# Grouped-query attention inside a fused encoder layer: both key-value heads in one piece, scores and products with v on alternating halves of the TensorE array

## The reference, cut to what matters

```python
def sink_attention(q, k, v, valid, sinks):
    s = jnp.einsum('...qhgd,...khd->...hgqk', q, k,
                   preferred_element_type=jnp.float32) * (ATTN_HEAD_DIM ** -0.5)
    if valid is not None:
        s = jnp.where(valid[..., None, None, None, :], s, -jnp.inf)
    sink = sinks.astype(jnp.float32).reshape(ATTN_KV_HEADS, ATTN_GROUP, 1, 1)
    m = jnp.maximum(jnp.max(s, axis=-1, keepdims=True), sink)
    p = jnp.exp(s - m)
    w = p / (jnp.sum(p, axis=-1, keepdims=True) + jnp.exp(sink - m))
    return jnp.einsum('...hgqk,...khd->...qhgd', w.astype(v.dtype), v)
```

## Time and profile before

| | |
|---|---|
| median of 3 runs | 1014.32 us (1013.77 to 1015.25) |
| the profiled execution, its own time | 1015.18 us |
| its span, first to last instruction | 1013.5 us |
| mean granted TensorE clock | 0.996 |
| TensorE busy | 992.2 us, 98% of the span |
| VectorE, ScalarE, GpSimd busy | 62%, 39%, 8% |

### The profile page before, as it was taken

The page is one execution under the profiler, slowest core; times in us unless marked ns, Lnnn a source line. Parts: engine busy times, 40 slices in busy tenths (PEclk is TensorE's granted clock), DMA queues, the critical chain, the costliest instruction groups (busy, mean ns, idle before and its releaser), DMA issues.

```text
span 1013.5 us, 19083 instructions
## 1 busy us (share of the span) xinstructions
PE 992.2 (98%) x7220; PEld 960.9 (95%) x7220; DVE 632.5 (62%) x1244; ACT 399.7 (39%) x693; POOL 85.8 (8%) x140
## 2 busy tenths in 40 slices
PE   6999999999999999999999899999999999999997
PEld 5999989898999999999999899999999999999997
DVE  5545665766666643434548789724997369965762
ACT  4324433423343522222544455423454135443252
POOL 1022212112110000000001200000000000030000
PEclk9999999999999999999999999999999999999999
DMA  7434212212221222244702513521234213365211
GB/s 206 125 111 128 80 55 64 63 53 67 68 65 56 65 87 83 72 126 132 220 22 84 215 55 94 158 83 43 84 101 129 84 43 114 89 225 155 84 46 49
DMA packets 166197, 98.45 MB, mean 97 GB/s; under 512 B 14656, under 2 KB 162528, under 8 KB 165872
## 3 DMA queue, kind: packets, MB, share of 16 engines
q1 hardware_dynamic: 159904, 79.19, 27.6%
q0 software_dynamic: 4336, 16.67, 4.6%
q10 hardware_dynamic: 1888, 1.64, 0.5%
HBM read 86.79 MB, written 10.75 MB: 96 GB/s over the span
## 4 chain that ended last, share of the span: by engine, by line
PE 91%; DVE 4%; issue 2%; ACT 2%; DMA 1%; DVEq 0%; SPq 0%; ACTq 0%
PE acc L679 34%; PE acc L935 10%; PE acc L937 10%; PE acc L936 10%; PE small L935 6%; PE small L936 6%; PE small L937 6%; PE small L807 2%; PE small L822 2%; PE small L850 1%; PE small L854 1%; PE small L759 1%; PE small L852 1%; PE small L1088 1%; DMA x_row<-in_x_sample 1%
## 5 line engine op out<-in xcount | busy, mean ns | idle before, releaser
L679 PE MATMUL acc<-xh,whi 128*128 128x288 f32 x736 | 163.1, 303 | 1.6 <-DVE wlo L1599 1.5
L679 PE MATMUL acc<-xl,whi 128*128 128x288 f32 x736 | 157.4, 295 | 0.0
L679 PE MATMUL acc<-xh,wlo 128*128 128x288 f32 x736 | 157.1, 294 | 0.0
L1116 ACT ACTIVATE whi<-raw 128x1024 fp32r<-128x1024 f32 (+1 forms) x62 | 62.1, 1001 | 198.3 <-PE acc L679 198.3
L1599 DVE TENSOR_TENSOR wlo<-raw,whi 128x1024 fp32r<-128x1024 f32 (+1 forms) x64 | 74.3, 1162 | 81.1 <-ACT whi L1116 77.8
L679 PEld LDWEIGHTS acc<-xh,whi 128*128 128x128 f32 x736 | 116.8, 189 | 8.5 <-issue 7.4
L679 PEld LDWEIGHTS acc<-xh,wlo 128*128 128x128 f32 x736 | 118.1, 188 | 0.0
L679 PEld LDWEIGHTS acc<-xl,whi 128*128 128x128 f32 x736 | 118.0, 188 | 0.0
L1906 DVE TENSOR_TENSOR wlo<-raw,whi 128x512 fp32r<-128x512 f32 (+2 forms) x93 | 81.0, 872 | 49.6 <-ACT whi L1327 33.8
L935 PE MATMUL acc<-yh,whi 128*128 128x288 f32 x360 | 107.2, 298 | 1.3 <-DVE wlo L1906 1.3
L937 PE MATMUL acc<-yh,wlo 128*128 128x288 f32 x360 | 106.1, 295 | 0.0
(11 more groups left out here) (312 smaller groups left out, 2376.9 us busy)
## 6 DMA issues: line engine op xcount, KB each, us to landing
raw<-in_w_in SPq DMA_DIRECT2D x92, 256.0 KB, 3.2
raw<-in_w_ffn_gate SPq DMA_DIRECT2D x44, 256.0 KB, 3.4
raw<-in_w_ffn_up SPq DMA_DIRECT2D x44, 256.0 KB, 4.0
raw<-in_w_ffn_down SPq DMA_DIRECT2D x32, 256.0 KB, 3.6
res<-x_scratch POOLq DMA_DIRECT2D x16, 288.0 KB, 4.3
raw<-in_w_branch_ret SPq DMA_DIRECT2D x16, 256.0 KB, 2.9
raw<-in_w_out SPq DMA_DIRECT2D x16, 256.0 KB, 4.4
raw<-in_w_ffn_down SPq DMA_DIRECT2D x16, 192.0 KB, 3.6
```

The costliest lines, as they stand in the source:

```text
L679: ins = nc.tensor.matmul(acc[:, a, hf, 0:HALF], w[:, s, at:at + P], x(k)[:, hf * HALF:(hf + 1) * HALF], start=first and n == 0 and m == 0, ...
L1116: nc.scalar.activation(whi[:, s, 0:n], raw[:, s, 0:n], ACT.Copy).then_inc(hi_ready, 1)
```

## The change

A round of pieces now takes two query heads of both key-value heads (round `p`: query heads 2p and 2p+1 of each). The score tiles stand in the order head 0, head 1, head 0, head 1, so that successive matmuls contract over partitions 0 to 63 and 64 to 127 in turn; head 0's scores go to the first bank of `att`, head 1's to the second. The products with v are two matmuls for each tile of keys, of half the moving columns, one to output partitions 0 to 63 and one to 64 to 127. ScalarE takes the result out in one copy over 128 partitions and half the columns. VectorE's reads of the sinks are re-indexed. The table `PLACES` and all semaphores' counts stay.

```diff
--- before.py
+++ after.py
@@ -792,20 +792,25 @@
             for n in (2, 3):
                 run_unit(unit(U_Q + n), unit(J_Q + n), (xh, xl))
 
-            def att_piece(piece, g, b):
-                n = 2 * b + g
+            def att_piece(piece, p, b):
+
+
+                n = 2 * b + p
                 nq, k0, k1, tiles = block_size(b)
                 if piece == "A":
-                    if isinstance(b, int) and b == 0 and g == 0:
+                    if isinstance(b, int) and b == 0 and p == 0:
                         pe.wait_ge(va_rows, 2)
                     pe.wait_ge(att_staged, b + 1)
                     if isinstance(b, int) and b == RH:
                         pe.wait_ge(cache_staged, 1)
                     wait(pe, att_out, n)
                     wait(pe, v_rows, 2 * b)
-                    for j in range(GROUP):
-                        ins = nc.tensor.matmul(att[0:nq, j * KW + k0:j * KW + k1], q_st[64 * g:64 * g + 64, j, 0:nq],
-                                               k_st[64 * g:64 * g + 64, k0:k1], start=True, stop=True)
+                    for j in range(2):
+                        for g in range(KV):
+                            slot = 2 * g + j
+                            ins = nc.tensor.matmul(att[0:nq, slot * KW + k0:slot * KW + k1],
+                                                   q_st[64 * g:64 * g + 64, 2 * p + j, 0:nq],
+                                                   k_st[64 * g:64 * g + 64, k0:k1], start=True, stop=True)
                     ins.then_inc(att_score, 1)
                 elif piece == "B":
                     pe.wait_ge(att_prob, n + 1)
@@ -819,8 +824,10 @@
                     pe.wait_ge(att_t0, n + 1)
                     pe.wait_ge(att_t1, n + 1)
                     for t, nk in tiles.items():
-                        ins = nc.tensor.matmul(att[64 * g:64 * g + 64, 0:GROUP * nq], v_st[0:nk, t, 64 * g:64 * g + 64],
-                                               prob_t[0:nk, t, 0:GROUP * nq], start=t == min(tiles), stop=t == 1)
+                        for g in range(KV):
+                            ins = nc.tensor.matmul(att[64 * g:64 * g + 64, 0:2 * nq], v_st[0:nk, t, 64 * g:64 * g + 64],
+                                                   prob_t[0:nk, t, 2 * g * nq:2 * (g + 1) * nq],
+                                                   start=t == min(tiles), stop=t == 1)
                     ins.then_inc(att_pv, 1)
 
             def ret_piece(piece, c, r, slot):
@@ -1184,9 +1191,9 @@
                         act.sem_inc(att_t0, 1)
                 elif piece == "C":
                     act.wait_ge(att_pv, n + 1)
-                    src = att[64 * g:64 * g + 64, 0:GROUP * nq].rearrange("p (j n) -> p j n", j=GROUP)
+                    src = att[:, 0:2 * nq].rearrange("p (j n) -> p j n", j=2)
                     settled()
-                    nc.scalar.activation(o_att[64 * g:64 * g + 64, :, span(P * b, nq)], src, ACT.Copy).then_inc(att_out, 1)
+                    nc.scalar.activation(o_att[:, 2 * p:2 * p + 2, span(P * b, nq)], src, ACT.Copy).then_inc(att_out, 1)
 
             def head_job(t, h):
 
@@ -1679,8 +1686,12 @@
             dve.wait_ge(sinks_ready, 1)
             dve.wait_ge(tables_in, 32)
 
-            def att_piece(piece, g, b):
-                n = 2 * b + g
+            def sink_of(p, slot):
+
+                return GROUP * (slot // 2) + 2 * p + slot % 2
+
+            def att_piece(piece, p, b):
+                n = 2 * b + p
                 nq, k0, k1, tiles = block_size(b)
                 if piece == "A":
                     dve.wait_ge(att_score, n + 1)
@@ -1691,13 +1702,14 @@
 
                         nc.vector.tensor_tensor_reduce(
                             out=prob[0:nq, j, k0:k1], in0=att[0:nq, j * KW + k0:j * KW + k1], in1=mcol, scale=SCALE,
-                            scalar=sinks[0:nq, GROUP * g + j:GROUP * g + j + 1], op0=ALU.add, op1=ALU.max,
+                            scalar=sinks[0:nq, sink_of(p, j):sink_of(p, j) + 1], op0=ALU.add, op1=ALU.max,
                             accum_out=top[0:nq, j:j + 1]).then_inc(dve_top, 1)
                     dve.wait_ge(dve_top, 6 * n + 4)
                     nc.vector.tensor_scalar(neg_top[0:nq, :], top[0:nq, :], -1.0, None, ALU.mult).then_inc(dve_top, 1)
                     dve.wait_ge(dve_top, 6 * n + 5)
-                    nc.vector.tensor_tensor(top[0:nq, :], sinks[0:nq, GROUP * g:GROUP * (g + 1)], neg_top[0:nq, :],
-                                            ALU.add).then_inc(att_top, 1)
+                    pair = sinks[0:nq, :].rearrange("p (g j) -> p g j", g=KV)[:, :, 2 * p:2 * p + 2]
+                    nc.vector.tensor_tensor(top[0:nq, :].rearrange("p (g j) -> p g j", g=KV), pair,
+                                            neg_top[0:nq, :].rearrange("p (g j) -> p g j", g=KV), ALU.add).then_inc(att_top, 1)
                 elif piece == "N":
                     dve.wait_ge(att_exp, n + 1)
                     nc.vector.tensor_tensor(den[0:nq, :], den[0:nq, :], sink_exp[0:nq, :], ALU.add).then_inc(dve_top, 1)
```

## The result

The changed kernel takes 1001.0 us (median, 1000.66 to 1001.56), the one before 1014.48: a ratio of 0.9867, 95% interval 0.9855 to 0.9879.

The account below looks back on a forecast made before the run. TensorE was taken to bound the kernel; partial overlap of halves would save 9.5 us in score and v pieces (scores 3.89 + 0.98, v 3.82 + 0.42 + 0.38), giving a median of 1004.8 us, range 1001.5 to 1014.9.

Parts of the forecast that it names:

- The ScalarE copy: Copy of the attention result, 64x512 to 128x256: from 0.59 to 0.385 us, 0 for the end.
- VectorE's waits for scores: Sign in the changed kernel's timeline: VectorE's waits for L807 should shrink by some 0.6 for each piece.
- no wait for `wlo`: Sign: new waits on L679 for `wlo` would have to appear if pieces shrink and the time doesn't.
- five slots where eight stood: Score and v pieces: starts in program order let halves overlap partly, 9.5 us less on TensorE; chance 0.58.
- 8 loads (0.87) leave nothing to gain: Block 0's score pieces: slot 0.112, one load 0.109, so 0 gained and the piece still takes 1.09 us.
- rival (1): Score and v pieces: halves fully independent, pairs overlap completely, -14.2 us, 1000.1 us; chance 0.07.
- (2): Only one kind of piece overlaps: scores alone 1009.6 us, v alone 1009.7 us; chance 0.13.
- (3): No overlap: the array takes fp32 records one after another whatever half; +0.15, 1014.5 us; chance 0.14.
- (4): Slower: no overlap, and each change of half exposes the load behind it; +4.5, 1018.8 us; chance 0.08.

Follow-up runs that it names:

- grouped order: Changed kernel with both matmuls of head 0, then both of head 1, inside each score and v piece; 1002.58 us, ratio 0.9877.
- the row and the column runs: Changed kernel with both heads' scores contracted over partitions 0 to 63: 1008.37 us; changed kernel with both heads' v products written to output partitions 0 to 63: 1007.92 us.
- three-to-one run: Changed kernel with three of a piece's four v products sent to output partitions 0 to 63 and one to 64 to 127; 1003.54 us, once.
- the kernel with both edits: Changed kernel with all scores contracted over the same rows and all v products in the same columns; 1015.41 us, ratio 1.0009 to the kernel before.
- Four quarters: Changed kernel, block 4's score pieces only: each key-value head's second query head writes to output partitions 64 to 127; 998.77 us, one time only.
- one shape: Changed kernel with block 4's v products always over 128 rows, zeros below the 64 keys: 1000.31 us; with each head's matmuls together as well: 1000.80 us.

## Why the prediction was wrong

**What held.** TensorE bounds the stretch, and what leaves a piece leaves the end: the pieces' own times (6 of block 1's kind and 2 each of blocks 0 and 4) sum to 9.3 us of scores and 8.7 of products with v after, 16.6 and 15.5 before, 14.1 us less, and the span is 14.3 less (spans of the kernel before differ by 2 us among themselves, so the 0.2 tell nothing). The ScalarE copy went to 0.386 us where 0.385 was said; VectorE's waits for scores shrank by 7.3 us; no wait for `wlo` appeared.

```profile
L1196 ACT ACTIVATE o_att<-small 128x256 f32 x6 | 2.3, 386 | 7.9 <-PE small L828 7.9
```

**What failed** is one step of the sum, in two places. "With starts in order, the sequence is A, then A with B, then B with A, then A with B, then B: five slots where eight stood": there are four. I took the order of starts in a trace where no neighbours used different halves, so where it could not have been otherwise, for a rule that holds between halves. The grouped order shows that it does not: each half goes through its own matmuls, past up to three records of the other that have not started. So 9.5 us were summed where the pieces lost 14.1. The second place is block 0, "8 loads (0.87) leave nothing to gain": I read 0.109 us as the time of one load on a single path that all loads share. Loads of the two halves run side by side, and block 0's score piece fell from 1.09 to 0.65, less than the 0.87 of eight loads one after another.

That was rival (1), to which I gave 0.07: 7.4 of scores and 6.8 of products with v said by its bound, 7.3 and 6.7 in the pieces' sums, 1000.1 us said and 1001.0 measured. Its bound was worked out correctly from rows of before; what was wrong was the argument that set it aside. Two small readings of the prediction are off without weight: 123.80 - 123.66 is 0.14, not 0.13, and block 4's v records step by 0.109 us, not 0.112.

**The other rivals.** (2) falls with the row and the column runs, each kind overlaps in full. The rule of the Trainium skill quoted there (TensorE: Matmul & The Clock Gate, "The mechanism": a load goes ahead of a running matmul only when the row group differs) is not borne out: in the v pieces both halves use all rows, and the loads are hidden all the same (steps of 0.216 us with a load in each). The same part also lets a load go ahead when it targets the background weight buffer, and with that the trace agrees. The same part states that matmuls start and end in program order; for the starts, between halves, the grouped and the three-to-one run show otherwise. Its span model, the time of one with about 4 ns for each further tile, fits if both records of an fp32 matmul are put for the one: the pairs here lie 7 ns apart. Two such pairs are four slots; the five that the prediction gave by it come from its program order, taken record by record. (3) is what the kernel with both edits does, 1015.4 us. (4) did not happen: a change of half costs nothing, only a change of shape does, as block 4 shows in the grouped order.

Still open: whether three records not yet started are always the most that a half can pass. That is read from three arrangements, and nothing longer was built to test it. The trace also doesn't say which half a record belongs to; that the pairs are one of each half is read from the runs in which both used the same half and no pair formed, and from the longer first record of each half.

## What to carry to other kernels

Matmuls that use 64 rows or 64 columns of the array are worth spreading over both halves even in fp32: price the piece as its fullest half, with its loads, and take neither a start order nor a common load path from a trace in which all neighbours used the same part. Balance between the halves counts. The order inside a piece counts little as long as each half's next matmul stands within reach (two fp32 matmuls of the other half could be passed, three could not). What does cost is a change of the array's shape, about 0.09 us and an exposed load each, and nothing overlaps across it. So group by shape, and pad a short key tile if that keeps the shape.

## What the runs showed of the hardware that was not expected

- Two halves of the array, by rows or by columns, each work through their own fp32 matmuls and weight loads at once: pairs within 0.01 us, and 0.215 us from pair to pair for the 256 columns of blocks 1 to 3.
- Four quarters do too: the score piece of 64 queries fell to 0.49 us from 0.80 for two halves and 1.44 for one.
- A half runs ahead of the program's order: with both of head 0's matmuls first, the piece grew by 0.01 us. It does so only so far: with three of the other half's first, it waited 0.49 us although it was free.
- The semaphore increment of the last matmul in the program does not come before the other half is done: the copy that waits for it started 0.22 us behind the fuller half's end, and 0.60 behind the end of that matmul itself.
- Nothing overlaps across a change of the array's shape: four groups of two records took 1.44 us where one shape took 0.59.
- Column halves that read the same moving partitions lose nothing by it: the v piece took 1.01 us, of which 0.05 + 4 x 0.216 + 0.09 explain 1.00.
